# Two more pairs per layer computed with seven half-size products instead of eight, in a two-layer streaming encoder step

## The reference, cut to what matters

```python
def _conv_ffn(h, conv_prev, w_up, conv_w, conv_b, w_down):
    uv = jnp.einsum('bld,df->blf', h, w_up)           # w_up: 1024 x 5632
    u, gate = uv[..., :D_FF], uv[..., D_FF:]          # D_FF = 2816
    u_ext = jnp.concatenate([conv_prev.astype(u.dtype), u], axis=1)
    uc = conv_b + sum(conv_w[j] * u_ext[:, j:j + seq] for j in range(CONV_W))   # CONV_W = 3
    y = jnp.einsum('blf,fd->bld', jax.nn.gelu(uc, approximate=False) * gate, w_down)
    return y, u_ext[:, seq:]
```

## Time and profile before

| | |
|---|---|
| median of 3 runs | 1576.74 us (1575.12 to 1579.2) |
| the profiled execution, its own time | 1573.91 us |
| its span, first to last instruction | 1572.2 us |
| PE busy | 1541.9 us, 98% of the span |
| DVE, ACT, POOL busy | 75%, 49%, 32% |

### The profile page before, as it was taken

The page is one execution under the profiler, slowest core; times in us unless marked ns, Lnnn a source line. Parts: engine busy times, 40 slices in busy tenths (PEclk is TensorE's granted clock), DMA queues, the critical chain, the costliest instruction groups (busy, mean ns, idle before and its releaser), DMA issues.

```text
span 1572.2 us, 41384 instructions
## 1 busy us (share of the span) xinstructions
PE 1541.9 (98%) x17631; PEld 1502.5 (96%) x17631; DVE 1181.6 (75%) x2011; ACT 776.0 (49%) x1390; POOL 496.0 (32%) x378
## 2 busy tenths in 40 slices
PE   8999999999999999999999999999999999999997
PEld 7999999989999999999999999998999999999997
DVE  4589646678769988898647894567786799888974
ACT  5455355655425444444444634556553344454445
POOL 5345432223323222222234354122233322222211
PEclk9999999999999999999999999999999999999999
DMA  5222210012333322332232222000223233323312
GB/s 161 68 72 76 81 43 5 4 23 82 100 88 94 96 81 82 104 97 70 71 99 68 81 79 77 11 4 4 62 79 97 81 98 96 91 81 96 95 53 89
DMA packets 219896, 115.45 MB, mean 73 GB/s; under 512 B 10356, under 2 KB 217474, under 8 KB 219714
## 3 DMA queue, kind: packets, MB, share of 16 engines
q1 hardware_dynamic: 219634, 112.79, 25.4%
q10 hardware_dynamic: 80, 0.02, 0.0%
HBM read 109.27 MB, written 3.53 MB: 72 GB/s over the span
## 4 chain that ended last, share of the span: by engine, by line
PE 93%; DVE 4%; issue 1%; ACT 1%; DMA 0%; SPq 0%; DVEq 0%; ACTq 0%
PE ps L783 26%; PE ps L784 26%; PE ps L1362 7%; PE ps L1363 7%; PE ps L1364 7%; PE ps L1033 2%; PE ps L1036 2%; PE ps L1030 2%; PE ps L995 1%; PE ps L1007 1%; PE ps L1098 1%; PE ps L788 1%; PE ps L1305 1%; PE ps L927 1%; PE ps L802 1%
## 5 line engine op out<-in xcount | busy, mean ns | idle before, releaser
L665 POOL TENSOR_TENSOR wlo<-raw,whi 128x1024 fp32r<-128x1024 f32 (+1 forms) x105 | 254.7, 2426 | 409.8 <-ACT whi L1474 409.8
L760 POOL TENSOR_TENSOR wlo<-raw,whi 128x512 fp32r<-128x512 f32 x96 | 141.5, 1475 | 414.7 <-ACT whi L1954 414.7
L1474 ACT ACTIVATE whi<-raw 128x1024 fp32r<-128x1024 f32 (+1 forms) x106 | 105.4, 994 | 274.8 <-PE ps L784 266.4
L783 PE MATMUL ps<-xh,whi 128*128 128x288 f32 x608 | 181.5, 299 | 2.3 <-DVE xl L2087 1.8
L784 PE MATMUL ps<-xh,whi 128*128 128x288 f32 x608 | 178.9, 294 | 0.0
L783 PE MATMUL ps<-xh,wlo 128*128 128x288 f32 x608 | 178.9, 294 | 0.0
L783 PE MATMUL ps<-xl,whi 128*128 128x288 f32 x608 | 178.8, 294 | 0.0
L784 PE MATMUL ps<-xh,wlo 128*128 128x288 f32 x608 | 178.7, 294 | 0.0
L784 PE MATMUL ps<-xl,whi 128*128 128x288 f32 x608 | 178.5, 294 | 0.0
L783 PEld LDWEIGHTS ps<-xh,whi 128*128 128x128 f32 x608 | 114.1, 188 | 4.5 <-issue 3.1
L784 PEld LDWEIGHTS ps<-xh,whi 128*128 128x128 f32 x608 | 114.2, 188 | 0.2
(11 more groups left out here) (381 smaller groups left out, 5062.7 us busy)
## 6 DMA issues: line engine op xcount, KB each, us to landing
raw<-in_ffn_w_up SPq DMA_DIRECT2D x88, 512.0 KB, 3.9
raw<-in_w_in SPq DMA_DIRECT2D x52, 512.0 KB, 3.8
Ei<-in_ffn_w_down SPq DMA_DIRECT2D x64, 256.0 KB, 3.3
raw<-in_w_out SPq DMA_DIRECT2D x16, 512.0 KB, 4.0
raw<-in_ffn_w_down SPq DMA_DIRECT2D x16, 256.0 KB, 2.8
xin<-in_x_prompt SPq DMA_DIRECT2D x4, 512.0 KB, 7.1
Ei<-in_ffn_w_down SPq DMA_DIRECT2D x16, 128.0 KB, 3.4
out<-xin SPq DMA_DIRECT2D x8, 256.0 KB, 2.9
```

Of the source, the lines that this page charges most:

```text
L665: e.tensor_tensor(wlo[s][:, 0:width], raw[s][:, 0:width], whi[s][:, 0:width].bitcast(F32), ALU.subtract).then_inc(w_lo[s], 1)
L760: lo = e.tensor_tensor(by_tile(D_lo[name]), A[name], by_tile(D_hi[name]).bitcast(F32), ALU.subtract)
L783: e.matmul(acc(out)[:, 0], lhsT, rhs[:, 0:HT], start=start, stop=stop)
L1474: e.activation(whi[s][:, 0:width], raw[s][:, 0:width], ACT.Copy).then_inc(w_hi[s], 1)
```

## The change

The list `FOLDS` takes the place of the number `PLAIN`: pairs 2, 4 and 6 to 21 are folded, pairs 0, 1, 3 and 5 are plain. So four pairs of the program more are folded (two in each layer), and there are three places in a layer where a plain pair is followed by a folded one: 1 to 2, 3 to 4 and 5 to 6. The order on ACT and DVE there is written anew: before pairs 4 and 6 DVE makes the four sums ahead of the value tile `up`; before all three, S1's hi part comes ahead of `conv_first` on ACT, and S1's lo part ahead of the gate tile `hf` on DVE. In a folded pair that follows a plain one, the sums of the next folded pair come first.

```diff
-PLAIN = 6
+FOLDS = [2, 4] + list(range(6, FF))
...
-                    if f > PLAIN:
+                    if f - 1 in FOLDS:
                         sp.wait_ge(d_sum, nth(SUMS, folded(l, f - 1), "S4"))
...
-                for f in range(PLAIN):
-                    for s in range(2):
-                        split(s, turn(s, l, PAIRS["ffn"] + f), KT * P)
-                for f in range(PLAIN, FF):
-                    for name in ("A11", "A12", "A22"):
-                        quad_rest(f, name)
+                for f in range(FF):
+                    if f in FOLDS:
+                        for name in ("A11", "A12", "A22"):
+                            quad_rest(f, name)
+                    else:
+                        for s in range(2):
+                            split(s, turn(s, l, PAIRS["ffn"] + f), KT * P)
...
+                def plain_up(f):
+
                     k = [turn(s, l, PAIRS["ffn"] + f) for s in range(2)]
                     if f >= 2:
                         for s in range(2):
                             down_hi(*mixed_down(f), s)
...
+                    if f + 1 in FOLDS:
+                        for name in AC_D:
+                            quad_hi(f + 1, name)
+                        conv_first(f)
+                        quad_hi(f + 1, "A12")
+                        quad_hi(f + 1, "A22")
+                        gelu(f)
+                    else:
+                        tile(0, k[0])
+                        conv_first(f)
+                        gelu(f)
+                        tile(1, k[1])
+                        inner_hi(f)
+
+                def folded_up(f):
+
+                    k = [turn(s, l, PAIRS["ffn"] + f) for s in range(2)]
+                    more = f + 1 in FOLDS
                     copy_b(f)
                     if more:
                         quad_hi(f + 1, "A11")
...
                     move_v(f)
+                    if f - 1 not in FOLDS:
+                        inner_hi(f - 1)
                     down_hi(*mixed_down(f), 0)
                     copy_c(f)
...
+                    else:
+                        split(0, k[0] + 1)
                     conv_first(f)
                     if more:
                         quad_hi(f + 1, "A22")
+                    elif f + 1 < FF:
+                        tile(1, k[1])
                     gelu(f)
...
-                    fold = f == PLAIN - 1
+                    fold = f + 1 in FOLDS
...
+                    finish_cycle(f - 1)
                     pad(f)
+                    if fold and f > 2:
+                        for name in SUMS:
+                            quad_sum(f + 1, name)
...
                     keep_last(f)
+                    if fold and f <= 2:
+                        for name in SUMS:
+                            quad_sum(f + 1, name)
                     if fold:
-                        for name in SUMS:
-                            quad_sum(PLAIN, name)
+                        for name in ("S2", "S3", "S4"):
+                            quad_lo(f + 1, name)
                     conv_rest(f)
                     if fold:
-                        for name in ("S2", "S3", "S4"):
-                            quad_lo(PLAIN, name)
+                        quad_lo(f + 1, "S1")
...
                     e.tensor_tensor(by_half(hf[:, :]), acc(PS[1]), by_half(nrs[:, :]), ALU.mult).then_inc(psum_free[1], 1)
-                    if fold:
-                        quad_lo(PLAIN, "S1")
                     gated(f, 1.0)
...
-                    m, more = folded(l, f), f + 1 < FF
+                    m, more = folded(l, f), f + 1 in FOLDS
                     own = [turn(s, l, PAIRS["ffn"] + f) + 1 for s in range(2)]
-                    if f == PLAIN:
-                        add_down(*mixed_down(f - 1), 0)
-                    add_down(*mixed_down(f - 1), 1)
-                    inner_lo(f - 1)
+                    if f - 1 in FOLDS:
+                        finish_cycle(f - 1)
                     if more:
                         for name in SUMS:
                             quad_sum(f + 1, name)
+                    if f - 1 not in FOLDS:
+                        finish_cycle(f - 1)
+                        inner_lo(f - 1)
...
+                def finish_cycle(f):
+
+                    if f in FOLDS:
+                        add_down(*mixed_down(f), 1)
+                        inner_lo(f)
+                    elif f >= 2:
+                        for s in range(2):
+                            add_down(*mixed_down(f), s)
```

More of the change, by code:

```diff
@@ L111, in folded @@
 def folded(l, f):
[L113 removed]
+    return l * len(FOLDS) + FOLDS.index(f)
 def mixed_down(f):
@@ L1414, in _ @@
                 for f in range(FF):
-                    if f < PLAIN:
+                    if f in FOLDS:
+                        folded_up(f)
+                    else:
                         plain_up(f)
-                    else:
-                        folded_up(f)
                     if f == 2:
@@ L1933, in quad_hi @@
                     k = [turn(s, l, PAIRS["ffn"] + f - 1) + 1 for s in range(2)]
-                    if f == PLAIN and name in ("A11", "S1"):
+                    plain = f - 1 not in FOLDS
+                    if plain and name in ("A11", "S1"):
                         ac.wait_ge(tile_done[0], k[0])
-                    elif f == PLAIN and name in ("A12", "A22"):
+                    elif plain and name in ("A12", "A22"):
                         ac.wait_ge(tile_done[1], k[1])
-                    elif f == PLAIN:
+                    elif plain:
                         ac.wait_ge(xm_lo, (l + 1) * FH)
@@ L1974, in conv_first @@
                     ac.wait_ge(f_gelu, t)
-                    if f < PLAIN:
+                    if f not in FOLDS:
                         ac.wait_ge(psum_free[0], turn(0, l, PAIRS["ffn"] + f) + 1)
@@ L2011, in copy_c @@
                     e.activation(bank_c, bank_b, ACT.Copy).then_inc(d_copy, 1)
-                for f in range(PLAIN - 1):
+                def plain_up(f):
                     k = [turn(s, l, PAIRS["ffn"] + f) for s in range(2)]
@@ L2037, in _ @@
                         quad_hi(f + 1, "A11")
-                    else:
-                        split(0, turn(0, l, PAIRS["ffn"] + FF), DW)
+                    elif f + 1 == FF:
+                        split(0, k[0] + 1, DW)
                     down_hi(*mixed_down(f), 1)
                     move_v(f)
+                    if f - 1 not in FOLDS:
+                        inner_hi(f - 1)
                     down_hi(*mixed_down(f), 0)
@@ L2046, in _ @@
                             quad_hi(f + 1, name)
-                    else:
-                        ac.wait_ge(d_prod, nth(PE_D, folded(l, f), "P2"))
-                        split(1, turn(1, l, PAIRS["ffn"] + FF), DW)
+                    elif f + 1 == FF:
+                        ac.wait_ge(d_prod, nth(PE_D, folded(l, f), "P2"))
+                        split(1, k[1] + 1, DW)
+                    else:
+                        split(0, k[0] + 1)
                     conv_first(f)
@@ L2056, in _ @@
                     inner_hi(f)
+                for f in range(FF):
+                    if f in FOLDS:
+                        folded_up(f)
+                    else:
+                        plain_up(f)
                 added(l, PAIRS["ffn"] + FF, (l + 1) * NORMS, DW, 0 if l == DEPTH - 1 else KT * P, True)
@@ L2835, in down_rest @@
                                     ALU.subtract).then_inc(e_lo[s], 1)
+                def finish_cycle(f):
+                    if f in FOLDS:
+                        add_down(*mixed_down(f), 1)
[3 more added lines that the diff above has]
+                            add_down(*mixed_down(f), s)
                 for f in range(FF):
-                    if f < PLAIN:
+                    if f in FOLDS:
+                        folded_up(f)
+                    else:
                         plain_up(f)
-                    else:
-                        folded_up(f)
-                add_down(*mixed_down(FF - 1), 1)
-                inner_lo(FF - 1)
+                finish_cycle(FF - 1)
                 add_tiles(PAIRS["ffn"] + FF, (l + 1) * NORMS)
```

5 lines of the change are left out of this document (1 added, 4 removed).

## The result

The changed kernel takes 1587.89 us (1586.33 to 1587.99, 4 runs) against 1575.93 for the old one in the same series: ratio 1.0071, 95% interval 1.0059 to 1.0084. It is 12 us slower. The forecast was 1578.8 with a range to 1585.0: wrong.

A forecast was written before the change was run, and what follows sets the result against it. TensorE, busy 98% of the span, was taken as the bound, so only fewer matmuls or gaps help. -6.3 - 7.0 + 9.0 + 5.8 + 0.6 = +2.1 us moves the median from 1576.7 to 1578.8 us, range 1572.0 to 1585.0.

The forecast's parts named there:

- The saved matmuls: On TensorE's path, four pairs fall from 96 to 84 matmuls, at 0.132 us each: -6.3 us.
- The S1 chain at pair 2: Step from pair 1 to 2: TensorE waits at P5 for S1's rest, +9.0 us over both layers (7.8 to 10.2).
- the upper of my two cases: One or two POOL turns hold DVE ahead of S1's rest, 8.1 or 9.3 us after the first sum; upper is two.
- Step 3 to 4 and 5 to 6 at P5: At P5 of pairs 4 and 6, S1's rest is ready 1.6 to 4 us early, so no wait.
- c22 at pair 6: TensorE waits for c22 ahead of P4 of pair 6, 2.9 us per layer (1.8 to 4.7): +5.8 us.
- My reading that DVE would stand idle for the load: In pair 6 DVE idles several us until `raw[1]` for pair 7 lands; the additions and `inner_lo` wait too.
- c22 at pairs 2 and 4: A split full tile on ACT and POOL makes c22 0.15 us late in each: +0.6 us, bounds 0 and 1.2.
- The granted clock: Slower rival, chance 0.2: after waits of 3.3 to 5.7 us TensorE falls to 1.2 GHz, +1.6 to +9.6 us, 1583.5.
- the signs of being wrong that the forecast named: Pair 2's wait 2 us or less, pair 7's sums right after pair 5's `gated` steps, or a granted clock dip.
- VectorE's overrun: Slower rival, chance 0.07: extra DVE work in pairs 3 and 5 delays S1's rest before pairs 4 and 6, +8.8 us, 1587.5.

The follow-up runs named there:

- e7: e5 with pair 2 plain again (pairs 4 and 6 to 21 folded): 1573.11 us, 0.9977 of the old kernel.
- e4: Changed kernel with DVE making the two additions ahead of the sums for pair 7 in pair 6: 1587.49 us, 1.0078 of the old kernel.
- e9: The changed kernel run again without any change, for a second trace: 1582.97 us in one execution.
- e5: Changed kernel with the sums for pair 7 moved behind c22 in pair 6: 1585.55 us, 1.0057 of the old kernel.
- e13: Changed kernel plus 24 unused matmuls of 8 columns between P1 and P5 of pair 2, layer 0 only: 1582.45 us, 1.0043 of the old kernel.
- e14: e11 plus 24 unused matmuls of 8 columns ahead of P4 of pair 2, layer 0 only: 1570.22 us, 0.9967 of the old kernel.
- e12: e7 with two of pair 7's sums ahead of c22, behind the additions, and two behind it: 1569.49 us, 0.9957 of the old kernel.
- e6: e5 with the step from pair 1 to 2 reordered, S1's hi and lo parts first: 1575.69 us, 0.9990 of the old kernel.
- e2: Changed kernel plus 28 unused filler matmuls in the wait between P1 and P5 of pair 2: 1580.39 us, 1.0033 of the old kernel.
- e11: e6 with two of pair 7's sums ahead of c22, behind the additions, and two behind it: 1572.92 us, 0.9979 of the old kernel.
- e1: Changed kernel plus unused matmuls in TensorE's waits, 28 at pair 2 and 12 at pair 6: 1577.97 us, 1.0020 of the old kernel.

## Why the prediction was wrong

**The saved matmuls** (-6.3): right, 48 instructions less. New waits of 15.4 us were forecast (9.0 + 5.8 + 0.6) and 15.0 measured, by the mechanism that was given for each.

**The S1 chain at pair 2** (ready 4.5 to 5.7 late in layer 0, 3.3 to 4.5 in layer 1): right. TensorE idled 5.18 and 4.08. DVE's timeline of the changed kernel in pair 1 shows each link:

```profile
411.55 0.69 DVE L2713 TENSOR_TENSOR Tall<-raw 128x512 f32<-128x512 f32 x1 [2.04 <-DMA raw<-in_ffn_w_up]
...
416.22 0.82 DVE L2740 SCALAR_TENSOR_TENSOR cv<-up,par,cv 128x578 f32<-128x578 f32 x1 [0.24 <-ACT cv L1981]
417.08 1.70 DVE L2743 SCALAR_TENSOR_TENSOR cv<-up,par,cv 128x578 f32<-128x578 f32 x1
418.70 1.75 DVE L2718 TENSOR_TENSOR wlo<-Tall,whi 128x512 fp32r<-128x512 f32 x1
```

The first sum waits for the load, the first convolution step comes 4.7 later, and each of the next two instructions lasts 0.9 to 1.1 longer than it should: POOL's two turns, the upper of my two cases.

**Step 3 to 4 and 5 to 6 at P5** (nothing): right, there is no such wait; e7 confirms it for pair 4.

**c22 at pair 6** (2.9 per layer): 2.35 and 2.70 of idle time, right. My reading that DVE would stand idle for the load held (the sums start at 487.63 after 4.33 idle), and the experiments add what I had not seen: the additions cost nothing there, because they stood in the shade of POOL's turn. What sets c22 is the landing plus 6.6 to 6.9 us (e4: sums from 487.96, c22 done at 494.53; changed kernel: 487.63 and 494.48).

**c22 at pairs 2 and 4** (+0.6, bounds 0 and 1.2): the list of waits has no row there. The low bound.

**The granted clock**: the step that failed. The forecast held it as a rival with 2 chances in 10 and put the price at 1.6 to 4.8 us for a fall, only at pair 2. It came with all four waits, those of 2.35 and 2.70 at pair 6 included, and cost 7.8 us: 5.0 at pair 2, near that rival's middle, and 2.8 at pair 6, where no fall was priced. (A slot does not quite double: 0.24 us against 0.132.) The reason given against it, that the old kernel waited 2.1 us with a full clock, was one execution's observation of two waits, and the earlier trace rows, from which the full clock was read, is too coarse to show a fall at all. e9 shows that the same wait of 2.4 us comes with and without a fall, and e5 and e7 had falls after 1.75 us. What the old trace could say was that a fall had not happened, not that it could not. A dip of the granted clock was among the signs of being wrong that the forecast named, and it is the one that came.

The rule of the Trainium skill that the forecast named ("TensorE: Matmul & The Clock Gate", Part 1: an idle TensorE goes back to half its clock) was borne out, though not after every wait (e9). The forecast's clock rival, 1583.5, was nearer than the forecast itself. The rival with the nearest number, VectorE's overrun at 1587.5, is near by luck: its waits ahead of pairs 4 and 6 never came.

**The token mixer of layer 1** (not in the forecast at all): +3.8 us in the first trace, +3.2 in the second. The second step that failed: the forecast has no term for it and gives no reason; the change doesn't touch that code. That it goes with the number of TensorE instructions ahead of it is shown by e13 and e14, one trace each. By what path (how the instructions reach the engine, for one) is open: no run tells that apart.

The sum closes to half a microsecond: -6.3 - 7.0 + 15.0 + 7.8 + 3.8 + 0.3 = +13.6 for spans that differ by 14.1. Without the clock, the mixer and the 0.3 it would be +1.7, where the forecast said +2.1. So the sign of the forecast came from the listed terms; the rest of the 12 us came from two that it left out or held for unlikely. Over all runs the clock cost somewhat less than in the two profiled executions: an estimate from the mean granted clocks, 0.9915 against 0.996, gives 2 x 0.0045 x 1587 = 14 us more at half clock, which at 0.45 is 6 us of the 12.

## What to carry to other kernels

On a TensorE that is 98% busy, price a new wait at its length plus the half clock that may follow: here 1.4 to 2.5 us for each wait of 2.4 to 5.2, as much as 11 to 19 matmuls saved. Make a wait that can't be avoided short, or split it: e12, with none over 1.3 us in the FFN, had no fall in its trace, and turned 12 us lost into 7 won by that and by not folding pair 2. Don't read a full clock off one execution, nor off a page whose digits are means of 40 us. Before explaining a difference of a few us, cut the trace at fixed marks, and look at the stretches that the change doesn't touch.

## What was unexpected

- The clock fell after waits as short as 1.75 us (e5, e6, e7), and did not fall after 2.54 (e13, pair 6 in layer 0), 2.41 (e2), 2.37 and 2.39 (e9) or 2.06 and 2.12. TensorE then worked at half the clock for 3.2 to 5.6 us. In several traces the fall came up to 1.5 us after TensorE had resumed.
- In e14 the clock fell in layer 0 at 426.5 with no idle time listed there: ahead of it TensorE had done the 24 matmuls of 8 columns, from 423.57 to 426.17, in place of most of the wait. In e11, without them, it stayed full after 1.55 us of idle time at that place. One trace each, so what the small matmuls did to the clock is not shown.
- The same kernel spreads: e1, with its waits half filled, ran from 1576.4 to 1581.4 us, and its two slowest runs (1581.4 and 1580.7) have its lowest mean granted clock, 0.995.
- A stretch of 415 us is 3.2 to 4.4 us longer in all six traces (the changed kernel twice, e4, e5, e6, e11) with 24 matmuls fewer ahead of it in layer 0, and 415.3 and 415.4 us when 24 dummies bring the count back.
- Work without a use can be worth its while: e1 has 80 matmuls more than the changed kernel and is 9 us faster, some 3.6 of it in the stretch.
